# Output gate projections of the mixer issued between the heads instead of in the state loop

## The reference, cut to what matters

```python
proj = h @ w_in
q_pre, k_pre, v, o_pre, i_pre, f_pre, u = jnp.split(proj, PROJ_SPLITS, axis=-1)
...
hm = mlstm(q, k, vv, li, lf)
hm = hm * lax.rsqrt(jnp.mean(hm * hm, axis=-1, keepdims=True) + RMS_EPS)
hm = hm.reshape(B, S, D_MLSTM) * norm_mlstm.astype(f32)
hm = jax.nn.sigmoid(o_pre.astype(f32)) * hm
...
g = jax.nn.gelu(ys)
ys = g * jax.nn.sigmoid(g @ w_glu.astype(f32))
mixed = jnp.concatenate([hm, ys], axis=-1).astype(h.dtype)
return mixed @ w_out
```

## Time and profile before

| | |
|---|---|
| median of 3 runs | 1480.25 us (1479.22 to 1481.89) |
| the profiled execution's own time | 1480.46 us |
| its span (first to last instruction) | 1478.4 us |
| PE busy | 1346.0 us, 91% |
| DVE busy | 467.6 us, 32% |
| ACT busy | 278.6 us, 19% |
| mixer of layer 0, state loop and tail, about | 72 to 188 us |
| mixer of layer 1, state loop and tail, about | 437 to 553 us |
| experts' layer | from 553 us to the end |

### The profile page before, as it was taken

The page is one execution under the profiler, slowest core; times in us unless marked ns, Lnnn a source line. Parts: engine busy times, 40 slices in busy tenths (PEclk is TensorE's granted clock), DMA queues, the critical chain, the costliest instruction groups (busy, mean ns, idle before and its releaser), DMA issues.

```text
span 1478.4 us, 18652 instructions
## 1 busy us (share of the span) xinstructions
PE 1346.0 (91%) x7760; PEld 761.4 (52%) x7760; DVE 467.6 (32%) x1049; ACT 278.6 (19%) x511; POOL 98.0 (7%) x115
## 2 busy tenths in 40 slices
PE   3998879999798886999999999999999999987775
PEld 2765469999785544545445444444433343332321
DVE  6787785555559734022010010101011110100002
ACT  2272234444236200000010100101101001100001
POOL 4240000000343000000000000000000000000000
PEclk9999989999999997999999999999999999999999
DMA  9243055544421208789999959898999999999994
GB/s 283 78 132 132 36 186 207 178 163 150 172 79 65 100 30 354 257 344 409 413 413 411 414 210 418 336 411 337 416 410 412 413 410 414 412 411 416 410 413 203
DMA packets 126734, 423.50 MB, mean 286 GB/s; under 512 B 21632, under 2 KB 23864, under 8 KB 118456
## 3 DMA queue, kind: packets, MB, share of 16 engines
q1 hardware_dynamic: 126648, 422.27, 73.4%
HBM read 421.20 MB, written 1.05 MB: 286 GB/s over the span
## 4 chain that ended last, share of the span: by engine, by line
PE 71%; DMA 14%; DVE 9%; ACT 2%; SPq 2%; issue 2%; POOL 0%; DVEq 0%; ACTq 0%
PE psall L2251 13%; DMA m_ring<-in_moe_w_down_dram 12%; PE psall L2342 11%; PE psall L2265 7%; PE psall L2280 6%; PE psall L1969 3%; PE psall L2353 3%; PE psall L2182 3%; PE psall L2184 3%; PE psall L2183 3%; PE psall L2129 2%; PE psall L2062 2%; PE psall L2228 2%; PE psall L2315 2%; PE psall L2381 2%
## 5 line engine op out<-in xcount | busy, mean ns | idle before, releaser
L2265 PE MATMUL psall<-m_ring,xeT 128*64 128x448 f32 x1024 | 204.2, 547 | 23.0 <-DMA m_ring<-in_moe_w_up_dram 23.0
L2342 PE MATMUL psall<-m_ring,hidT 128*64 128x512 f32 (+1 forms) x672 | 201.0, 597 | 16.0 <-DMA m_ring<-in_moe_w_down_dram 15.1
L2251 PE MATMUL psall<-m_ring,xeT 128*128 128x448 f32 x512 | 195.7, 543 | 0.8 <-DVE xeT L1834 0.8
L2265 PEld LDWEIGHTS psall<-m_ring,xeT 128*64 128x64 f32 x1024 | 74.0, 137 | 141.1 <-issue 139.9
L2251 PEld LDWEIGHTS psall<-m_ring,xeT 128*128 128x128 f32 x512 | 97.3, 191 | 94.1 <-issue 92.9
L2342 PEld LDWEIGHTS psall<-m_ring,hidT 128*64 128x64 f32 (+1 forms) x672 | 72.8, 154 | 135.0 <-issue 119.3
L1856 DVE TENSOR_TENSOR hid<-e_silu,psall 64x448 f32<-64x448 f32 x32 | 19.9, 623 | 354.7 <-ACT e_silu L1216 352.8
L2280 PE MATMUL psall<-m_ring,xeT 128*32 128x448 f32 x1024 | 102.0, 542 | 0.0
L1559 DVE TENSOR_TENSOR w_lo<-ring,w_hi 128x1024 fp32r<-128x1024 f32 x66 | 80.5, 1225 | 68.0 <-ACT w_hi L1171 68.0
L2182 PE MATMUL psall<-hnT_hi,w_hi 128*128 128x256 f32 x352 | 99.6, 283 | 1.2 <-DVE hnT_lo L1692 1.2
L2184 PE MATMUL psall<-hnT_hi,w_lo 128*128 128x256 f32 x352 | 99.5, 283 | 0.0
(11 more groups left out here) (326 smaller groups left out, 1475.2 us busy)
## 6 DMA issues: line engine op xcount, KB each, us to landing
m_ring<-in_moe_w_gate_dram SPq DMA_DIRECT2D x128, 896.0 KB, 20.0
m_ring<-in_moe_w_up_dram SPq DMA_DIRECT2D x128, 896.0 KB, 17.1
m_ring<-in_moe_w_down_dram SPq DMA_DIRECT2D x64, 1792.0 KB, 19.0
ring<-in_w_in_dram SPq DMA_DIRECT2D x10, 2048.0 KB, 12.9
ring<-in_ffn_w_gate_dram SPq DMA_DIRECT2D x5, 2048.0 KB, 10.4
ring<-in_ffn_w_up_dram SPq DMA_DIRECT2D x5, 2048.0 KB, 7.8
ring<-in_ffn_w_down_dram SPq DMA_DIRECT2D x5, 2048.0 KB, 7.9
ring<-in_w_out_dram SPq DMA_DIRECT2D x4, 2048.0 KB, 8.3
```

Source lines behind the costliest of these rows:

```text
L2251: ins = M(m_bank(key)[:, 0:MH], x[:, i, 0:P], weights(kind, i, s), start=(i == 0), stop=(i == KT - 1))
L2265: ins = M(m_bank(key)[64 * n:64 * n + 64, 0:MH], x[:, i, 0:64], weights(kind, i, s), start=(i == 0), stop=(i == KT - 1))
L2342: ins = M(y, hidT[:, r, 0:shape[0]], rows(r, 512 * n, 512), **ends)
```

## The change

The two gate projections leave steps 6 and 7 of the state loop and go into the tail: o 0 between the scores of head 1 and z 0, o 1 between the scores of head 3 and the numerator of head 2. On ACT, their tanh moves too: the first behind `dec_exp(1)`, the second behind `dec_exp(2)`. The products themselves are the same.

```diff
 def mixer_steps(l):
     return [[("qk", l, 0)], [("qk", l, 1)], [("y", l, 0), ("qk", l, 2)], [("qk", l, 3)], [("y", l, 1), ("v", l, 0)],
-            [("v", l, 1), ("tr", l)], [("y", l, 2), ("o", l, 0)], [("o", l, 1)]]
+            [("v", l, 1), ("tr", l)], [("y", l, 2)], []]
...
-    order = [("mu", l, 0), ("mu", l, 1), ("sc", l, 0), ("sc", l, 1), ("z", l, 0), ("z", l, 1), ("num", l, 0),
-             ("mu", l, 2), ("sc", l, 2), ("num", l, 1), ("mu", l, 3), ("sc", l, 3), ("num", l, 2), ("os", l, 0, 0),
+    order = [("mu", l, 0), ("mu", l, 1), ("sc", l, 0), ("sc", l, 1), ("o", l, 0), ("z", l, 0), ("z", l, 1), ("num", l, 0),
+             ("mu", l, 2), ("sc", l, 2), ("num", l, 1), ("mu", l, 3), ("sc", l, 3), ("o", l, 1), ("num", l, 2), ("os", l, 0, 0),
              ("ss", l), ("num", l, 3), ("os", l, 0, 1), ("os", l, 1, 0), ("os", l, 1, 1)]
...
-            (lo if kind in ("z", "num", "os") else hi)(n, "A" if kind in ("z", "ss", "hmT") else "V")
+            (lo if kind in ("z", "num", "os") else hi)(n, "A" if kind in ("o", "z", "ss", "hmT") else "V")
...
+            def gate_out(l, t):
+                arrived(act, ("o", l, t))
+                nc.scalar.activation(o_gate[:, t, :], bank(("o", l, t))[:, :], ACT.Tanh,
+                                     scale=0.5).then_inc(drained["A"], 1)
...
                 dec_exp(l, 1)
+                gate_out(l, 0)
                 for i in range(2):
                     arrived(act, ("z", l, i))
...
                 dec_exp(l, 2)
+                gate_out(l, 1)
```

More of the change, by code:

```diff
@@ L1114, in mixer @@
                                                  ACT.Copy).then_inc(drained["A"], 1)
-                        elif n[0] == "v":
+                        else:
                             nc.scalar.activation(v_aug[:, n[2], :, 0:DH], v3(src, NH),
                                                  ACT.Copy).then_inc(drained["A"], 1)
-                        else:
-                            nc.scalar.activation(o_gate[:, n[2], :], src, ACT.Tanh,
-                                                 scale=0.5).then_inc(drained["A"], 1)
                     if q + 2 < COUPLES:
@@ L1971, in channels, with tokens @@
                 return ins
+            def tokens(n):
+                kind, l, t = n
+                chunk_wait(pe, (kind, l))
+                open_bank(pe, n)
+                for k in range(KT):
+                    ins = M(bank(n)[:, :], hnT[:, k, t * P:(t + 1) * P], v3(chunk((kind, l)), KT)[:, k, :],
+                            start=(k == 0), stop=(k == KT - 1))
+                done(ins)
             def mixer(l):
@@ L2058, in mixer @@
                         else:
[L2059 to L2064, removed]
+                            tokens(n)
                     if q + 2 < COUPLES:
@@ L2069, in mixer @@
                     kind = n[0]
-                    if kind == "mu":
+                    if kind == "o":
+                        tokens(n)
+                    elif kind == "mu":
                         open_bank(pe, n)
```

## The result

The changed kernel took 1501.07 us (median of 4 runs, 1497.48 to 1501.75) against 1480.74 us: a ratio of 1.0133, 95% interval 1.0114 to 1.0152. It is slower, by 20.3 us, where 16.2 us more (1496.5) was forecast and 1491.5 to 1501 was the range. So the time lies at the very end of the range: the direction came out, and the main cost with it, the size was some 4 us short. The profiled execution took 1501.75 us, its span is 1499.8 us.

A forecast was written before the change was run, and what follows sets the result against it. PE was taken to bound the tail, tied with DVE in the loop: 28.4 us of matmuls, less earlier starts (3.73), holes (2.94, 2.95) and os 0 0's low clock (3.5), plus 3.9 low clock, gave 16.2 more: 1496.5 us, range 1491.5 to 1501.

The forecast's parts named there:

- The tail has few holes, so the projections cost there what they hid before: Tail on PE: about 14 us of matmuls per layer find about 4 us of holes; 28.4 us moved in all.
- The tie at y 3, and DVE's wait behind the gate's tanh: Loop's end: projections and DVE's couple 7 both hold y 3; without DVE's wait it starts 1.73 and 2.00 us earlier.
- The hole ahead of head 2 and the low clock of os 0 0 are taken off: Tail: o 1 covers PE's waits of 2.94 and 2.95 us; os 0 0 takes 3.43 us instead of 5.13.
- Low clock after the empty loop, 4.7 us: From y 3 on: 13 us of PE idling leaves 1.2 GHz for 4.7 us after restart, costing 3.9 us in all.
- the clock stays low longer: Rival, after the loop: low clock lasts 8.3 us, slowing o 0 by 1.8 us per layer; 1500.1 us, chance 0.13.
- From the numerator of head 3 on nothing is shorter, and nothing longer either: End of each tail: PE rows follow one another, so delays of 8.25 and 7.98 us at head 3 just shift onward.
- Weights in time, experts' layer as long as before: Later weight loads still land with over 8 us of cover in layer 0; experts' layer only shifts; cost nothing.

The follow-up runs named there:

- e5: The changed kernel with only the first of the eight products of each gate projection, order and waits kept: 1479.50 us, ratio 0.9994.
- e6: The changed kernel with o 0 moved on to o 1, both ahead of the numerator of head 2: 1499.99 us, ratio 1.0138.
- e3: The changed kernel with o 0 kept in step 6 of the state loop, only o 1 in the tail: 1488.52 us, ratio 1.0051.
- e7: The kernel before with only ACT's order changed, the gate's two tanhs behind the GELU's tanh of the same step: 1481.34 us, ratio 1.0007.
- e1: The changed kernel plus 16 never-read 128x512 matrix products in steps 6 and 7 of each layer's state loop: 1493.78 us, ratio 1.008.
- e2: The changed kernel with o 0 ahead of mu 0, first in the tail, its tanh ahead of `dec_exp(0)`: 1504.88 us, ratio 1.0154.
- e4: On top of e3, 320 of o 1's 512 columns in step 7 of the loop, 192 ahead of the numerator of head 2: 1477.50 us, ratio 0.9970.
- e8: On top of e4, mu 0 and mu 1 issued ahead of y 3 instead of behind it: 1476.21 us, ratio 0.9976.

## Why the prediction was right, and where it was short

- *The tail has few holes, so the projections cost there what they hid before.* Right: e5 (take the work out, and the cost goes), e6 (the place doesn't matter), e3 (the first finds the hole, the second next to nothing).
- *The tie at y 3, and DVE's wait behind the gate's tanh.* Right to a tenth: y 3 1.83 us earlier in layer 0 of the changed kernel (1.73 forecast) and 2.09 in layer 1 (2.00 forecast); and e7 shows the other side of the tie.
- *The hole ahead of head 2 and the low clock of os 0 0 are taken off.* Right as a row: no idle time, 3.44 us against the 3.43 forecast. But the forecast booked the 1.7 and 2.0 us as gone because the hole was filled. In e7 layer 0 and in e5 the clock stayed up in os 0 0 with a hole of 2.94 and 2.08 us ahead of it, and in e7 the loss came in the os row behind instead. So what brings the fall to one row or the other isn't shown, and in the changed kernel it wasn't saved but moved on (see the next but one).
- *Low clock after the empty loop, 4.7 us.* This term was mis-sized. It was taken from restarts behind 3 us of idle time where a projection or os followed 2.4 and 1.4 us later; it was 9.6 and 9.0 us. It cost 2.1 us more at z 0 in layer 0 and 1.8 in layer 1. Against e1 the whole low clock between y 3 and z 0 is 8.4 us in both layers together, where 3.9 were in the sum. The length of the idle time is not what was overlooked, since e3 has the same low stretch behind 4.84 us. The rival "the clock stays low longer" had named it, with 8.3 us for the duration and 1500.1 us for the time; it is nearest to what came.
- *From the numerator of head 3 on nothing is shorter, and nothing longer either.* This step failed. In the changed kernel the clock falls at the hole of 1.43 us, which it did not before: the numerator and the os row together take 12.54 us in layer 0 (170.95 to 183.49) where they took 11.04, and 13.90 us in layer 1 (543.68 to 557.58). In layer 0 it wasn't felt: hmT is 11.5 us late, but the row for which PE then waits for DVE (202.92) is only 9.99 us later than before, as late as the numerator of head 3 (10.01), from which DVE takes head 3, to go on to the gating of the heads, the S5 half of `x_res` and layer 1's S5 weights. So behind head 3 of layer 0 DVE sets the pace, and not one PE row after the other, as the prediction has it. The norm's transposes then ran at full speed, 1.97 us instead of 3.68, and the first product of the dense SwiGLU starts 213.52 - 204.79 - 0.48 = 8.25 us later than before, the forecast's number to the digit. That is luck: the low clock after the loop cost 1.8 us more at head 3 than forecast, and the low clock that the norm's transposes met in the kernel before was over by then here, which gave 1.7 us back. In layer 1 nothing was given back, and its total was 4.3 us above the forecast, 1.4 us up to the numerator of head 3 and 2.9 behind it. These are the 4 us that the sum is short.
- *Weights in time, experts' layer as long as before.* Right for the first, and nearly for the second: the norm ahead of the router is 20.70 us later than before, the end of the span 21.4 us.

What stays open is what makes the clock come back. In e2 the same projection behind the same y 3 met the full clock 3.1 us after the restart in one layer and 9.2 us after it in the other. It is open too what brings the fall at the small holes.

## What to carry to other kernels

Work that moves out of a stretch where another engine sets the pace costs its whole length, less the holes, wherever the engine that does it sets the pace; add up that engine's holes in the new place before anything else. A hole is best filled with a piece of its own size: 3/8 of one projection made the kernel faster (by 0.3%), two whole ones made it slower (by 1.3%). And an engine's filling may be worth keeping for the clock's sake even where it looks free to remove; in e5, where the low clock after the empty loop was made up in os 0 0, the kernel was as fast as before without it.

## What the runs showed of the hardware

- After the 13 us without matrix work TensorE stayed at 1.2 GHz for 9.6 and 9.0 us, through y 3, mu and the scores and into the projection; 28 us of useless products in the gaps (e1) took all of that away. Behind only 4.84 and 5.08 us without work (e3) it was 9.6 and 9.2 us, no less.
- In the traces of the changed kernel and of e2 to e6, the clock, once low, never came back while y 3, mu or the scores ahead of z 0 ran, whether the idle time had been 13, 5 or 0.7 us. It came back 0.1 to 6 us after a projection or z had begun.
- The clock also fell behind short gaps: in e4 during mu and the scores with two gaps of 0.7 us around y 3, and at a hole of 1.43 us, or in the row behind it, in both layers of the changed kernel and of e2, e3 and e8, in one layer of e1, e4, e6 and e7, and in none of e5 and the kernel before. So the same instructions with the same hole met the fall in one layer and not in the other. Where it falls moves from one order of the program to the next, even when only ACT's order changes (e7), and each of these falls cost the numerator of head 3 and the os row 1.4 to 3.0 us together.
